# One layer of a hybrid decoder: norm, latents, values and queries of the second and third token span, moved from a stage of their own ahead of the fetches to the head of each span's stage, between fetch units; ten buffers for fetched rows instead of nine

## The reference, cut to what matters

```python
h = rmsnorm(x, norm_mix)                      # x: 16 meta + 1024 prompt tokens, 8 x 4 sample tokens; D = 1024
B, C, xin, q_lat, kv_lat, kr_raw, gc, ga = split(h @ w_in)
u = C * xin;  conv_y = B * conv3(u)                            # 512 channels
ckv = rmsnorm(kv_lat)                         # 256 latents
kr  = rope(rmsnorm(kr_raw))                   # 32, shared by heads
cq  = rmsnorm(q_lat)                          # 384
q   = cq @ w_uq; qn = rmsnorm(q[:64]); qr = rope(rmsnorm(q[64:]))   # 8 heads
kn  = rmsnorm(ckv @ w_uk);  v = ckv @ w_uv
y_a = softmax(qn.kn + qr.kr) @ v              # causal; the sample tokens attend to 1024 paged keys
x  += (sigmoid(gc) * (conv_y @ w_conv_out) + sigmoid(ga) * (y_a @ w_attn_out)) @ w_mix_out
h2  = rmsnorm(x)
# experts: 8 heads, two 128-key searches, top 16 of the pairs -> 128 experts for each token
out = sum_k softmax(best)_k * gelu(expert_u[idx_k] . h2) * expert_v[idx_k]
x  += out
```

## Time and profile before

| | |
|---|---|
| median of 3 runs | 3591.35 us (3588.91 to 3599.55) |
| the profiled execution | 3590.14 us, span 3588.3 us from its first to its last instruction |
| first fetch issued | 529.1 us after the start |
| granted TensorE clock, mean | 0.902 of full speed |
| PE busy, share of the span | 84% |
| DVE, ACT, POOL busy | 71%, 38%, 30% |

### The profile page before, as it was taken

One profiled execution on the slowest core, in us unless ns is written; L12 is line 12 of the kernel. 1 busy time (PEld: TensorE's weight loads), 2 busy tenths in 40 slices (PEclk: granted clock), 3 DMA queues, 4 the chain that ended last, 5 costly groups with the idle time before them and its releaser, 6 DMA issues.

```text
span 3588.3 us, 33492 instructions
## 1 busy us (share of the span) xinstructions
PE 3027.4 (84%) x9652; PEld 1685.7 (47%) x9652; DVE 2551.2 (71%) x5686; ACT 1346.6 (38%) x3945; POOL 1088.7 (30%) x1252
## 2 busy tenths in 40 slices
PE   7988988687999998577878898899688988878877
PEld 4536875244555554233444444445245545455421
DVE  3233148987677789977677768789987777756864
ACT  2222114388322333465662222343344444413343
POOL 0000013333233234333343333333343333333342
PEclk9988999789999999788889999999798989867999
DMA  3213449999999999899999999999999999989998
GB/s 123 69 39 119 118 141 422 391 393 401 382 417 422 387 346 370 341 402 411 394 407 422 422 414 422 409 422 402 406 398 414 395 413 406 394 346 422 422 421 364
DMA packets 235102, 1274.62 MB, mean 355 GB/s; under 512 B 45198, under 2 KB 65486, under 8 KB 99366
## 3 DMA queue, kind: packets, MB, share of 16 engines
q0 software_dynamic: 152064, 1107.36, 75.6%
q1 hardware_dynamic: 81126, 160.72, 12.6%
q10 hardware_dynamic: 1728, 4.39, 0.3%
HBM read 1258.98 MB, written 13.40 MB: 355 GB/s over the span
## 4 chain that ended last, share of the span: by engine, by line
PE 32%; DVE 23%; DMA 22%; issue 7%; ACT 5%; POOL 1%; SPq 0%; DVEq 0%; POOLq 0%; ACTq 0%
DMA tl_uv<-in_uv,tl_idx 22%; PE tl_f L972 11%; DVE tl_uv L1570 9%; PE tl_f L1234 7%; DVE tl_acc L1551 4%; PE tl_f L1262 3%; PE tl_f L1178 3%; PE tl_f L1245 2%; PE tl_f L1033 1%; PE tl_f L1146 1%; PE tl_f L1097 1%; POOL tl_uv L903 1%; DVE tl_eq L1670 1%; PE tl_f L1169 1%; ACT L1309 1%
## 5 line engine op out<-in xcount | busy, mean ns | idle before, releaser
L903 POOL DMA_INDIRECT tl_uv<-in_uv,tl_idx x1056 | 1041.5, 986 | 1886.4 <-PE tl_f L972 1132.4
L1570 DVE CUSTOM_DVE_ANT_0 tl_uv<-tl_uv,tl_f 128x1024 f32<-128x1024 f32 x1056 | 1267.8, 1216 | 414.2 <-DMA tl_uv<-in_uv,tl_idx 396.8
L972 PE MATMUL tl_f<-tl_uv,tl_diag 128*128 128x512 f32 (+1 forms) x2460 | 1292.0, 667 | 299.8 <-ACT tl_diag L1281 292.8
L972 PEld LDWEIGHTS tl_f<-tl_uv,tl_diag 128*128 128x128 f32 (+1 forms) x2460 | 480.9, 207 | 957.3 <-issue 480.9
L1309 ACT ACTIVATE tl_ge<-tl_a 128x1 f32<-128x1 f32 x1056 | 210.5, 199 | 1253.2 <-DVE tl_a L1570 1201.6
L1551 DVE SCALAR_TENSOR_TENSOR tl_acc<-tl_uv,tl_w,tl_acc 128x1024 f32<-128x1024 f32 x433 | 554.8, 1281 | 71.3 <-ACT tl_w L1293 71.2
L1293 ACT ACTIVATE tl_w<-tl_ge,tl_weight 128x1 f32<-128x1 f32 x1024 | 301.5, 294 | 33.2
L1262 PE MATMUL tl_f<-H,w_tail 128*128 128x384 f32 (+2 forms) x1024 | 262.5, 411 | 7.0 <-DVE H L1895 6.8
L1281 ACT ACTIVATE tl_diag<-K,tl_w 128x128 f32<-128x128 f32 (+1 forms) x615 | 244.4, 397 | 45.2 <-PE tl_f L972 25.8
L1234 PE MATMUL tl_f<-H,w_tail 128*128 128x256 f32 (+2 forms) x768 | 235.7, 463 | 2.1 <-DVE tl_ya L1841 2.1
L1262 PEld LDWEIGHTS tl_f<-H,w_tail 128*128 128x128 f32 x1024 | 178.9, 193 | 102.8 <-issue 36.6
(11 more groups left out here) (244 smaller groups left out, 2884.8 us busy)
## 6 DMA issues: line engine op xcount, KB each, us to landing
w_tail<-in_w_merge SPq DMA_DIRECT2D x80, 512.0 KB
w_tail<-in_w_peer SPq DMA_DIRECT2D x64, 576.0 KB
w_tail<-in_w_conv SPq DMA_DIRECT2D x36, 512.0 KB
tl_uv<-in_uv,tl_idx POOLq DMA_INDIRECT x1056
w_tail<-in_w_mix SPq DMA_DIRECT2D x32, 512.0 KB
X<-in_cache SPq DMA_DIRECT2D x48, 128.0 KB
X<-in_x SPq DMA_DIRECT2D x8, 536.0 KB, 6.8
o_y<-tl_acc ACTq DMA_DIRECT2D x8, 512.0 KB
```

Of the source, the lines that this page charges most:

```text
L903: pool.indirect_dma_start(UV[:, u % RING, :], None, d["uv"], bass.IndirectOffsetOnAxis(ap=which, axis=0)).then_inc(landed[u % RING], 16)
L972: mm = pe.matmul(Y[0:m, half * 512:(half + 1) * 512], DG[:, (pe_count[u] - 1) % DIAGS, 0:m], UV[:, u % RING, D + half * 512:D + (half + 1) ...
L1570: dve.tensor_tensor_reduce(UV[:, u % RING, 0:D], UV[:, u % RING, 0:D], HP[:], 1.0, 0.0, ALU.mult, ALU.add, A[:, t % 2, i:i + 1]).then_inc( ...
```

## The change

- `CHUNKS` becomes one chunk of FRONT = 272 columns (16 meta tokens and the first span). `front_stage` and `query_stage` handle only these: 272 columns instead of 1072, three value tiles instead of nine, ten jobs instead of thirty. The remaining 800 columns of X are loaded in front_stage as eight DMAs that are queued ahead of the weights of latent blocks 2 to 5, and its end waits for them (`rest_in`).
- For c = 1 and c = 2 (`LAZY`) a new section `lazy` stands ahead of attention, on all engines. It makes the norm of the span's 384 columns (416 with the sample tokens for c = 2), its latents, values, keys and queries, and stores them to memory. The sample tokens' absorbed queries (ABSB) are made at the end of the one for c = 2.
- The keys and queries are now 20 jobs of 192 (or 208) columns, in four passes: two halves of the columns, keys (4 jobs), then queries (6). Their spread matmuls (JSPR) have one PSUM bank, where `back` had two.
- The section's buffers lie in space that is used otherwise later, so it has waits for its own stores: ACT waits at the third value tile for the store of the first, at job 0 for all stores of values and latents, at job 10 for the first key store, at job 14 for the first query store. SP issues the attention loads only when all stores of the section have landed.
- The nine or ten weight loads of the section (6 latent blocks and w_uv of 0.5 MB, 0.5 MB and 2 x 0.6 MB of w_head, 0.5 MB of w_ukT for c = 2) go through the three weight slots.
- Three small gains are loaded at the head of tail_stage. RING is 10; the scratch for the descriptors of indirect DMAs is halved.
- `TICK` of both stages gets the section's costs in front. The same units are now spread over more steps. Worked out from `due`, the unit at which each part starts:

| | section | attention | channels | merge | mix | rank | end of rank |
|---|---|---|---|---|---|---|---|
| stage 1 before | | 56 | 135 | 158 | 207 | 226 | 288 |
| stage 1 after | 56 | 87 | 156 | 176 | 219 | 235 | 289 |
| stage 2 before | | 296 | 461 | 495 | 566 | 594 | 684 |
| stage 2 after | 296 | 343 | 489 | 519 | 582 | 606 | 686 |

```diff
-CHUNKS = [(0, 360), (360, 360), (720, 352)]
+SPANS = [(0, 256), (256, 384), (640, 384), (1024, NS)]
+LAZY = (1, 2)
+FRONT = META + SPANS[LAZY[0]][0]
+CHUNKS = [(0, FRONT)]
...
-                sp.dma_start(X[:, k, :], d["x"][:, k, :]).then_inc(x_in[k // 2], 16)
+                sp.dma_start(X[:, k, 0:FRONT], d["x"][:, k, 0:FRONT]).then_inc(x_in[k // 2], 16)
...
+            for k in range(KD):
+                sp.dma_start(X[:, k, FRONT:], d["x"][:, k, FRONT:]).then_inc(rest_in, 16)
...
-RING, WRING, DIAGS = 9, 3, 4
+RING, WRING, DIAGS = 10, 3, 4
...
+        JOBS = [(p, j) for p in range(4) for j in (range(4) if p % 2 == 0 else range(4, NJ))]
+        NJOBS = len(JOBS)
+        PASS_FIRST = [JOBS.index((p, p % 2 * 4)) for p in range(4)] + [NJOBS]
...
+        def backs(n):
+            p, i = JOBS[n][0], n - PASS_FIRST[JOBS[n][0]]
+            if p == 0 or i < 2:
+                return range(0)
+            at, step = PASS_FIRST[p - 1], 1 if p % 2 else 3
+            return range(at + (i - 2) * step, at + (i - 1) * step)
...
+        lazy_order = lambda c: ([(c, NORM, 0), (c, LAT, 0)]
+                                + [x for b in range(1, NLAT) for x in [(c, LAT, b)] + [(c, LSUM, LAT_LAST.get(b - 1))] * (b - 1 in LAT_LAST)]
+                                + [(c, LSUM, 2)] + [(c, VAL, t) for t in range(TMAX)]
+                                + [x for n in range(NJOBS) for x in [(c, JOB, n)]
+                                   + [(c, JSUM, JOBS[n][0] - 1)] * (n in PASS_FIRST[1:]) + [(c, JSPR, m) for m in backs(n)]]
+                                + [(c, JSUM, 3)] + [(c, JSPR, m) for m in range(PASS_FIRST[3], NJOBS)]
+                                + [(c, ABSB, b) for b in range(2)] * (c == NCH - 2))
...
+                order += lazy_order(c) if c in LAZY else []
...
+        lazy_banks = {NORM: (3,), LAT: (0, 1, 2), LSUM: (3,), VAL: (0, 1, 2), JOB: (0, 1), JSUM: (2,), JSPR: (3,), ABSB: (0, 1)}
...
-        PRE = [len(x) + 5 + NCV for x in items] + [DEC]
-        TICK = [[6 + 2 * PARTS[c][1]] * len(items[c]) + [8] * 5 + [8] * NCV
+        ATT = [len(x) + 5 + NCV for x in items]
+        PRE = [n + (LSTEPS if c in LAZY else 0) for c, n in enumerate(ATT)] + [DEC]
+        LTICK = [12] + [10] * NLAT + [4] * TMAX + [3] * NJOBS + [6, 3]
+        TICK = [(LTICK if c in LAZY else []) + [6 + 2 * PARTS[c][1]] * len(items[c]) + [8] * 5 + [8] * NCV
                 + [8, 8, 4, 4] * KD + [12] + [8] * KD + [16] + [16] * HC + [8] * 4 + [0] for c in range(NCH - 1)]
...
+                col = slice(META + a, META + a + w)
...
+                sp.wait_ge(n_set, KD * (li + 1))
...
+                sp.wait_ge(ranked, c)
+                sp.dma_start(l_cs[:, :, 0:w], d["cossin"][:, :, col]).then_inc(l_in, 16)
+                for g in range(WRING, weights.ASK + 1):
+                    weight(g)
...
+                for t in range(TMAX):
+                    j, p = divmod(META + a + t * P, P)
+                    heads = l_v[:, t % 2].rearrange("p (h v) -> p h v", v=VH)
+                    sp.wait_ge(act_took, act_count[c, VAL, t])
+                    sp.dma_start(d["s_v"][:, p:P, j, :].rearrange("h p v -> p h v"), heads[0:P - p]).then_inc(v_kept[t % 2], 16)
+                    sp.dma_start(d["s_v"][:, 0:p, j + 1, :].rearrange("h p v -> p h v"), heads[P - p:P]).then_inc(v_kept[t % 2], 16)
+                weight(weights.ASK + 1)
...
+                for half in range(2):
+                    lo = a + half * (w // 2)
+                    m = min(w // 2, a + NMAX - lo)
+                    sp.wait_ge(j_set, 4 * li + 2 * half + 1)
+                    sp.dma_start(d["s_k"].rearrange("(j b) p n -> (b p) j n", b=2)[:, :, META + lo:META + lo + m],
+                                 j_raw[:, 0:4, 0:m]).then_inc(k_kept, 16)
+                    sp.wait_ge(j_set, 4 * li + 2 * half + 2)
+                    sp.dma_start(d["s_qn"].rearrange("(j b) p n -> (b p) j n", b=2)[:, :, lo:lo + m],
+                                 j_raw[:, 4:8, 0:m]).then_inc(q_kept, 16)
+                    sp.dma_start(d["s_qr"].rearrange("(j b) p n -> (b p) j n", b=4)[:, :, lo:lo + m],
+                                 j_raw[:, 8:10, 0:m]).then_inc(q_kept, 16)
+                    if half == 0 and w > NMAX:
+                        weight(weights.ABSORB)
+                if w > NMAX:
+                    sp.wait_ge(s_asked, 1)
...
+                sp.wait_ge(l_kept, 32 * (li + 1))
+                for i in range(2):
+                    sp.wait_ge(v_kept[i], 32 * (2 - i) * (li + 1))
+                sp.wait_ge(k_kept, 32 * (li + 1))
+                sp.wait_ge(q_kept, 64 * (li + 1))
...
+                if c in LAZY:
+                    lazy_loads(c, a)
...
+            def job_back(c, n, m):
+                p, j = JOBS[n]
+                if n == 0:
+                    pe.wait_ge(l_in, 48 * (nth(c) + 1))
+                if n == PASS_FIRST[p]:
+                    pe.wait_ge(j_inv, 4 * nth(c) + p + 1)
+                bank_free(c, JSPR, n)
+                pe.matmul(F[:, 3, 0:m], j_spread[:, j, :], j_root[:, p % 2, 0:m], start=True, stop=True).then_inc(proj, 1)
...
+            def lazy(c, a):
+                w, li = wide(c), nth(c)
+                m, at = w // 2, -PRE[c]
+                units(due(c, at, 0))
+                bank_free(c, NORM, 0)
+                for k in range(KD):
+                    pe.wait_ge(n_squared, KD * li + k + 1)
+                    mm = pe.matmul(F[:, 3, 0:w], K[:, C_MEAN:C_MEAN + P], n_sq[:, k % 2, 0:w],
+                                   start=(k == 0), stop=(k == KD - 1))
+                    mm.then_inc(n_summed if k < KD - 1 else proj, 1)
+                for b in range(NLAT):
+                    units(due(c, at + 1 + b, 0))
+                    s = arrived(weights.lazy(c, b))
+                    bank_free(c, LAT, b)
+                    for k in range(KD):
+                        if b == 0:
+                            pe.wait_ge(n_set, KD * li + k + 1)
+                        mm = pe.matmul(F[:, b % 3, 0:w], W[:, s, k, :], H[:, k, META + a:META + a + w],
+                                       start=(k == 0), stop=(k == KD - 1))
+                    mm.then_inc(proj, 1)
+                    if b:
+                        lazy_sum(c, b - 1, w)
...
+                for t in range(TMAX):
+                    units(due(c, at + 1 + NLAT + t, 0))
+                    if t == 0:
+                        lazy_sum(c, NLAT - 1, w)
...
+                for n, (p, j) in enumerate(JOBS):
+                    units(due(c, at + 1 + NLAT + TMAX + n, 0))
...
+                    if n == 4:
+                        pe.wait_ge(l_step, 13 * (li + 1))
...
+                    if n:
+                        job_sum(c, n - 1, m)
+                    for b in backs(n):
+                        job_back(c, b, m)
+                units(due(c, at + LSTEPS - 2, 0))
+                job_sum(c, NJOBS - 1, m)
+                for b in range(PASS_FIRST[3], NJOBS):
+                    job_back(c, b, m)
+                units(due(c, at + LSTEPS - 1, 0))
+                if c == NCH - 2:
...
+            def lazy(c, a):
...
+                units(due(c, at, LAG_ACT))
+                act.wait_ge(mset, c * KD)
+                for k in range(KD):
+                    if k >= 2:
+                        act.wait_ge(n_summed, (KD - 1) * li + k - 1)
+                    act.activation(n_sq[:, k % 2, 0:w], X[:, k, META + a:META + a + w], ACT.Square).then_inc(n_squared, 1)
+                act.wait_ge(proj, ready[c, NORM, 0])
...
+                for t in range(TMAX):
+                    units(due(c, at + 1 + NLAT + t, LAG_ACT))
+                    if t == 0:
+                        lat_root(2)
+                    act.wait_ge(proj, ready[c, VAL, t])
+                    if t >= 2:
+                        act.wait_ge(v_kept[0], 32 * (2 * li + 1))
+                    act.activation(l_v[:, t % 2, :], F[:, t % 3, :], ACT.Copy).then_inc(act_took, 1)
...
+                for n, (p, j) in enumerate(JOBS):
+                    units(due(c, at + 1 + NLAT + TMAX + n, LAG_ACT))
+                    act.wait_ge(proj, ready[c, JOB, n])
+                    if n == 0:
+                        act.wait_ge(l_step, 13 * (li + 1))
+                        act.wait_ge(l_kept, 32 * (li + 1))
+                        for i in range(2):
+                            act.wait_ge(v_kept[i], 32 * (2 - i) * (li + 1))
+                        if c == NCH - 2:
+                            act.wait_ge(s_kept, 32)
+                    if n == PASS_FIRST[2]:
+                        act.wait_ge(k_kept, 32 * li + 16)
+                    if n == PASS_FIRST[3]:
+                        act.wait_ge(q_kept, 64 * li + 32)
+                    if n >= 2:
+                        if closes(n - 2):
+                            act.wait_ge(proj, ready[c, JSUM, JOBS[n - 2][0]])
+                        else:
```

(26 more changed lines are left out.)

471 lines of the change are left out of this document (327 added, 144 removed).

## The result

| | |
|---|---|
| before, median of 4 runs | 3591.37 us (3588.91 to 3599.55) |
| after, median of 4 runs | 3656.39 us (3649.43 to 3661.11) |
| ratio | 1.0179, 95% interval 1.0163 to 1.0195 |
| the profiled execution of after | span 3654.6 us, mean granted clock 0.892 |
| predicted | 3630 us, range 3490 to 3705 |

The kernel became slower by 65 us in the median. The profiled spans differ by 66.3.

A forecast was written before the change was run, and what follows sets the result against it. It took TensorE's columns to bound the front, fetches attention and stage 2, and both PE and DMA stage 1's channels to mix. Terms -192 - 54 - 130 + 193 + 231 - 8 = +40 on 3590.1 gave 3630 us, range 3490 to 3705.

The forecast's parts named there:

- Front end: Parts ahead of the first fetch: bound by TensorE's columns, ending at 96.2 instead of 289.4 us; term -192, bounds -200 and -180.
- gain loads: Three loads on SP ahead of the first attention loads, 0.45 us each, giving 1.3 us back.
- Rest of the stages: Old parts of stages 1 and 2 with fewer units: -54 us in stage 1, -130 in stage 2.
- Section of stage 1: New section ahead of stage 1's attention: +193 us, of which PE works some 105.
- the clock: In each section, 8 us for a lower granted clock, since PE idles a good third of it.
- rival (a): Buffers and lags swallow the waits; sections cost PE work and fetches, 136 and 150 us: 3492 us, chance 0.25.
- Store waits: ACT waits in the sections for their own stores: 13 us for values in stage 1, 23 in stage 2, plus key and query waits.
- Tenth buffer: One more buffer for fetched rows: -8 us, ends 0 and -35, as landed rows shorten no PE and DVE chains.
- Merge unchanged: Sign in the changed profile: stage 1's merge unchanged, with PE over 95% busy.
- (c): Rival: stores pay full price, 27 us per value store and 13 for keys, sections 240 and 260: 3706 us, chance 0.13.
- (b): Rival: only the DMA engines count, 27 us for weights and 13 for stores, all else hides: 3430 us, chance 0.07.
- (d): Rival: near break-even, waits and ends a quarter shorter than priced: 3590 us, chance 0.10.

The follow-up runs named there:

- e1_ring9: The changed kernel with nine instead of ten buffers for fetched rows: 3671.45 us, ratio 1.0211 to the kernel before.
- l2_only: The changed kernel with the section for stage 2 alone, a front of 656 columns and ten buffers: 3589.34 us, ratio 0.9982 to the kernel before.
- e4_squares: The changed kernel with nine buffers, six norm squares on ACT ahead of the rank's last weights: 3664.78 us, ratio 1.0195 to the kernel before.
- e5_keys: The changed kernel with nine buffers and separate room for values, keys and queries, removing nearly all ACT store waits: 3630.93 us, ratio 1.0098 to before.

## Why the prediction was right, and where it was off

**Front end.** -192.0, and the mechanism as told: TensorE's columns set this part. That it fits to the microsecond is luck: the tail's first load is issued at 98.2 us, 2.0 later than predicted (the query stage's first product comes at 58.1 us, where 56 was said), and from there to the first fetch it is 0.8 us shorter than before (238.9 for 239.7) where 1.3 more was predicted for the gain loads.

**Rest of the stages.** -52.7 and -122.4 for -54 and -130. The windows of the earlier trace rows are cut at round times, not where the parts begin, so the single lengths that the prediction gives (185, 288, 218) can't be set beside the new ones; the differences can. Cut at the same products, attention, channels to mix and rank changed by -32.9, -11.2 and -8.6 us in stage 1 (-31, -10, -13 predicted) and by -67.8, -35.4 and -19.2 in stage 2 (-72, -42, -16). Each is within 7 us. But these rows hold the tenth buffer, for which the prediction had 8 us more, so the missing units alone gave back less than was said. The profile of e1_ring9, which has nine buffers as the kernel before (its longest run, 9 us over its median), has -41 and -119.

**Why moving costs time at all.** In stage 1 the moved work took 194 us and 31 fewer units gave back 53, 1.7 each; in stage 2 239 us and 47 units gave back 122, 2.6 each, the pace of the fetches. With nine buffers on both sides it is 1.3 and 2.5. Taking 800 columns out of the front gave 192. l2_only shows by a run that the larger loss is stage 1's (71 us against 18). That this is because PE was full there already (97% busy from channels to mix) fits the traces and was not tried by itself.

**Section of stage 1.** Predicted 18, 39, 10, 13, 71, 34 and 8 for the clock. Measured by the first instruction of each piece: norm and first block 27.7, latents 36, values 11, store wait 17.1, jobs 71.8, end 30.5. That 193.9 fits 193 is luck in part: the norm is 10 over and the store wait 4, the latents and the end are 3 under each, and the 8 do not appear. In stage 2 (239.2 for 231) norm and latents are 19 and 6 over (38.6 for 20, 52.7 for 47), and store wait, jobs and end together 8 under, the clock term apart. TensorE's own work was put at 105 us and is 131.7, near the 136 that rival (a) gave to work and fetches. A step of the end's chain of spreads was put at 1.85 us and is 1.51. The norm is the term that was mis-sized. Its cause in stage 2 stands in the timeline of the changed kernel, end of stage 1's rank:

```profile
1411.11 0.36 ACT L1799 ACTIVATE tl_weight<-tl_weight 128x192 f32<-128x192 f32 x1 [4.20 <-DVE tl_placef L1933]
...
1413.71 0.97 ACT L1646 ACTIVATE tl_gates<-X 128x416 f32<-128x416 f32 x2
...
1414.39 8.91 PE L1321 MATMUL tl_f<-tl_gates,K 128*128 128x416 f32 x16 [17.41 <-ACT tl_gates L1646]
```

PE is idle 17.4 us for the norm's squares, which stand on ACT behind the last weights of the rank, which wait for DVE's last top 16. In stage 1 the wait is 8.1 us, and the squares stand behind the gelu of a unit whose dot product DVE makes only after its last work for the rank. Before, attention's first scores came there and needed neither: the score at 1449.62 follows the last unit's product at once. The cover of the rank's tail was lost, and the prediction named no such wait. e4_squares, which makes six of the squares ahead, shortens this stretch by 11 us in its traces, for 6 in the time that are not clear of noise. The 8 us for the clock are no piece of their own in the trace: the granted clock is 0.79 in both sections, and what that costs lies inside the pieces (a pair of spreads takes 1.00 us in the end's chain and 0.59 among the jobs).

**Store waits.** In size right: PE idle 17.1 and 19.7 us where 13 and 23 were predicted, and by e5_keys 41 us in all for this and the key and query waits (65 predicted). The mechanism was wrong in its rate. DMA queues while ACT waits for the first value store:

```profile
DMA packets 3195, 7.26 MB, mean 399 GB/s; under 512 B 2128, under 2 KB 2416, under 8 KB 2433
...
q0 software_dynamic: 863, 6.24, 81.9%
q1 hardware_dynamic: 2332, 1.01, 19.7%
```

In these 18.2 us (579.2 to 597.4) SP's queue moved 2332 packets beside 863 of the fetches, 2.7 to one and 7.8 ns each, not one to one and 26 ns. In stage 2 it was 1438 beside 1033 in 20.2 us (1493.3 to 1513.5), 1.4 to one and 14 ns each. By these rates one store of 1024 packets would take 8 or 14 us; the first one took 17 us in stage 1 and 21 in stage 2. The latents' store lay in front of it and the next tile's packets behind it; how the rest divides between them no run shows. The rule of the Trainium skill that was weighed ("DMA: Bandwidth & Descriptors", "Queues, rings and completion order") counts turns between rows by packets and says that a packet can hold many descriptors; the fetches went on beside the stores, as turns would have it, but not at one record to one (2.7 and 1.4), and no run here shows how many records of the trace make one turn.

**Tenth buffer.** -8 predicted, -11 measured by e1_ring9 and -24 in the kernel before; the prediction's argument, that a landed row shortens no chain of PE and DVE, does not hold there. What the buffer gave in the changed kernel has no row of its own in the table; it lies in the rows of the stages. So the 26 us by which the sum of +40 fell short are 1 and 8 in the sections, 1 and 8 in the rest of the stages, and these 8.

**Signs that were named.** First fetch at 337: seen. Section of 190 us at a DMA share near 0.6: 193.9 and 0.64. PE under 65% busy: missed, 68%. ACT idle before the copies of jobs 0 and 10: seen, though the longest wait stood before the third value tile; before job 14 only 1.0 us, in stage 1. PE idle 25 to 35 us ahead of the first score: missed. The stretch is 30.5 us long with 10.75 of spreads in it, and the wait for the load that ends it is 11.6 us (4.7 in stage 2). Merge unchanged: channels to mix at 98% busy. What would have spoken against it (share over 0.9, stores in under 5 us, an attention that doesn't get shorter) did not come.

**The rivals.** The decision point of (a) was a section sum of 384 us; it is 433. (c) had the sections at 240 and 260, 46 and 21 us over. (b) and (d) are out by 226 and 66 us. What stays open: how the gain of a tenth buffer in the kernel before spreads over its stages, and what the smaller descriptor scratch costs.

## What to carry to other kernels

Work moved from a stage that waits for nothing into one that overlaps costs what the engine that is full there needs for it, and gives back only what the taken-out units cost where they stood: read that price for each stage (1.7 and 2.6 us here) before moving all of it. A section that reuses its own buffers waits for its own stores, and removing half of such waits can move the idle time to the next load behind them; remove all, then tune how much other work stands in it, in this order, because here the best amount changed with the waits. Ask of the first step of a moved section what it stands behind on each engine, as the norm's squares did here. Time the small part of a bundled change by itself: one more buffer alone was worth 24 us, and the whole bundle cost 65.
